# State-space steps and mLSTM steps of a hybrid token mixer in one loop

## The reference

```python
# SSD, per head: y = ((C B^T) * exp(segsum(a))) xc + C state * exp(a_cum)
#                state = state * exp(a_total) + B^T (decay * x)
# mLSTM, per head: m_t = max(b + m0, max(Dm)); W = exp(Dm - m_t)
#                num = (q k^T * W) v + (q C0) * exp(b + m0 - m_t); h = num / max(|den|, exp(-m_t))
#                C, n, m carried on to the next chunk
```

## Time and profile before

| | us |
|---|---|
| median of 3 runs | 4205.56 (4199.91 to 4212.05) |
| the profiled execution, own time | 4204.44 |
| its span | 4202.7 |
| PE / PEld / DVE / ACT busy | 3844.1 / 3257.1 / 2863.1 / 1994.6 |
| mean granted TensorE clock | 0.949 of full speed |

### The profile page before, as it was taken

The page is one execution under the profiler, slowest core; times in us unless marked ns, Lnnn a source line. Parts: engine busy times, 40 slices in busy tenths (PEclk is TensorE's granted clock), DMA queues, the critical chain, the costliest instruction groups (busy, mean ns, idle before and its releaser), DMA issues. The chain is left out here.

```text
span 4202.7 us, 61275 instructions
## 1 busy us (share of the span) xinstructions
PE 3844.1 (91%) x22686; PEld 3257.1 (78%) x22686; DVE 2863.1 (68%) x5816; ACT 1994.6 (47%) x4063; POOL 0.2 (0%) x4
## 2 busy tenths in 40 slices
PE   7999749989999999999999999989759899977998
PEld 4884547778887689999997788868449788867887
DVE  2535564348986868888768766654565499888666
ACT  2243213236666755555556544434224466665443
POOL 0000000000000000000000000000000000000000
PEclk9999869999999999999999999989769999999999
DMA  4221202225564455565554466523005355622665
GB/s 169 72 71 60 98 0 84 100 86 180 183 184 138 135 165 182 184 185 184 183 183 131 140 190 190 161 88 117 0 0 183 119 182 182 186 82 86 189 189 165
DMA packets 142200, 568.35 MB, mean 135 GB/s; under 512 B 15808, under 2 KB 17344, under 8 KB 130240
## 3 DMA queue, kind: packets, MB, share of 16 engines
q1 hardware_dynamic: 142016, 566.14, 42.7%
HBM read 565.03 MB, written 1.05 MB: 135 GB/s over the span
## 5 line engine op out<-in xcount | busy, mean ns | idle before, releaser
L1081 ACT ACTIVATE high<-ring 128x512 fp32r<-128x512 f32 x1632 | 1028.3, 632 | 1031.1 <-PE ps L515 510.1
L1538 DVE TENSOR_TENSOR low<-ring,high 128x512 fp32r<-128x512 f32 x1632 | 1075.8, 688 | 294.1 <-ACT high L1081 282.9
L515 PE MATMUL ps<-h_pair,high 128*128 128x512 f32 x3456 | 1236.1, 400 | 31.7 <-DVE low L1538 30.9
L515 PE MATMUL ps<-h_pair,low 128*128 128x256 f32 x3456 | 970.7, 281 | 0.0
L515 PEld LDWEIGHTS ps<-h_pair,high 128*128 128x128 f32 x3456 | 652.4, 189 | 188.0 <-issue 12.7
L911 PE MATMUL ps<-wt,high 128*128 128x512 f32 x2048 | 713.1, 392 | 5.7 <-DVE low L1538 5.7
L515 PEld LDWEIGHTS ps<-h_pair,low 128*128 128x128 f32 x3456 | 655.4, 190 | 0.0
L913 PE MATMUL ps<-wt,low 128*128 128x256 f32 x2048 | 574.7, 281 | 0.0
L515 PE MATMUL ps<-arena 128*128 128x128 f32 (+8 forms) x2432 | 444.3, 340 | 125.4 <-ACT arena L1081 75.6
L1081 ACT ACTIVATE arena<-ps 128x256 f32<-128x256 f32 (+3 forms) x654 | 271.1, 425 | 514.8 <-PE ps L515 486.1
L515 PEld LDWEIGHTS ps<-arena 128*128 128x128 f32 (+2 forms) x2432 | 326.3, 211 | 218.8 <-issue 115.7
(11 more groups left out here) (171 smaller groups left out, 4442.2 us busy)
## 6 DMA issues: line engine op xcount, KB each, us to landing
ring<-u_in SPq DMA_DIRECT2D x384, 512.0 KB, 3.6
ring<-v_in SPq DMA_DIRECT2D x384, 512.0 KB, 3.6
ring<-win_in SPq DMA_DIRECT2D x56, 1024.0 KB, 4.8
ring<-wmod_in SPq DMA_DIRECT2D x24, 1024.0 KB, 5.0
ring<-wq_in SPq DMA_DIRECT2D x48, 512.0 KB, 3.6
ring<-wmod_in SPq DMA_DIRECT2D x48, 512.0 KB, 3.6
ring<-wbr_in SPq DMA_DIRECT2D x16, 768.0 KB, 4.2
ring<-wout_in SPq DMA_DIRECT2D x8, 1024.0 KB, 4.8
```

What stands on the lines that cost most here:

```text
L515: return pe.matmul(o, l_, r, start=first, stop=last)
L1081: return act.activation(o, i_, f, **kw_)
L1538: return dve.tensor_tensor(o, a, b, op)
```

## The change

The SSD step and the mLSTM step of the same tile and direction stand in one loop body on every engine.

- Buffers: the SSD scratch gets a place of its own behind that of mLSTM; `dmat` has two halves, one per group, and is multiplied in place (`mmat` is gone); mLSTM adds up in `ml_acc`, which lies over `mlT`; the modulation rows go to `modrow_late`. `mergedT`, `br_high` and two of the three `w_high` buffers move.
- TensorE's order of a step: cb, row, ml_row, ml_qk, first half of modulation row A, ssd_dst, second half of A (and the turn of the row before), ssd_off, ml_int, ssd_y, first half of row B, ml_wT, second half of B, ml_num, ml_dst. `ssd_dst` is two products of 256 columns, each into 64 partitions of one half bank, in place of one of 512; so the state is read in two whole instructions in place of four half ones.
- ScalarE makes the SSD decays itself: relu(cm - row), four per group with a per-partition bias, then exp(-x). It takes the mLSTM exponentials in four pieces with the negative maximum as bias. It copies row A before the mLSTM exponentials, row B at the end of the step.
- VectorE multiplies `cb` by a 0/1 triangle as it reads it, has neither L1751 nor the subtraction on `rD`, and fewer instructions of 4 columns: the maxima carried from step to step are rearranged.
- The `ssd_dst` input `xd` is made first in the step.
- After the loop: both norms together, with one small instruction for all tiles where there were one per tile; the first gate slot is split at once, the second and third among the norms. The transposes of SSD come after the first gate slot's products, those of mLSTM after the second's. `br_high` of the attention follows the first slot's sigmoids, that of SSD the SSD transposes, that of mLSTM the second slot.

```diff
+        mergedT = view(scr_at, KB, T)
...
+        modrow_late = view(shapes_at + C_COS - C_KEPT, 2, 256)
...
+        ml_acc = view(s_mlT, NT, 512)
...
+        s_ssd = s + 4112
+        s = s_ssd
+        xc, xd, dmat, cb = view(s, 512), view(s + 512, 512), view(s + 1024, 2, 512), view(s + 2048, 256)
...
+        w_high = [rounded(f"w_high{r_}", w_, SLOT) for r_, w_ in enumerate((s_ssd, s_ssd + SLOT, merge_at))]
...
+                def rest_of_mod(n, hf):
                     if l == 0:
+                        w = slot(start["mod_rest", 0] - MOD_FIRST + n).rearrange("p (k m) -> p k m", k=KB)
+                        if hf == 0:
+                            row_bank[0] = claim("mod_row", 0, n)
+                        for k in range(4 * hf, 4 * hf + 4):
+                            i = mm(row_bank[0][0:2, 0:256], csil[:, k, :], w[:, k, :], k == 0, k == KB - 1)
+                        if hf:
+                            i.then_inc(*inc("mod_row", 0, n))
+                            if n > MOD_FIRST:
+                                mod_turn(0, n - 1, mod_bank[0], modrow_late)
...
+                            rest_of_mod(MOD_FIRST + 2 * (d * NT + n), 0)
+                        if kept_on:
+                            b = claim("ssd_dst", l, d, n)
+                            pe.wait_ge(*at("ssd_xd", l, d, n))
+                            pe.wait_ge(*at("B_t_read", l))
+                            for g in range(2):
+                                gp = slice(g * SN, g * SN + SN)
+                                i = mm(b[gp, 0:256], B_tm[:, t, gp], xd[:, g * 256:(g + 1) * 256])
+                            i.then_inc(*inc("ssd_dst", l, d, n))
+                        if shown:
+                            rest_of_mod(MOD_FIRST + 2 * (d * NT + n), 1)
...
+                            rest_of_mod(MOD_FIRST + 2 * (d * NT + n) + 1, 0)
                             b = claim("ml_wT", l, d, t)
                             pe.wait_ge(*at("ml_qk_read", l, d, t))
                             for h in range(MH):
                                 i = pe.transpose(b[:, h * P:(h + 1) * P], rW[:, h * P:(h + 1) * P], ident)
                             i.then_inc(*inc("ml_wT", l, d, t))
+                            rest_of_mod(MOD_FIRST + 2 * (d * NT + n) + 1, 1)
...
+                        if pr == 0 and q == 0:
+                            turn_out("ssd_T", "ssd_norm", acc)
+                        if pr == 0 and q == 1:
+                            turn_out("ml_T", "ml_norm", ml_acc)
...
+                            for g in range(2):
+                                b = bank("ssd_row", l, d, t, g)
+                                if shown_before:
+                                    act.wait_ge(*at("ssd_mm", l, *shown_before, g))
+                                for j in range(4):
+                                    h = d * 8 + g * 4 + j
+                                    i = fn(dmat[:, g, j * P:(j + 1) * P], b[:, j * P:(j + 1) * P], ACT.Relu,
+                                           scale=-1.0, bias=cm[:, t, h:h + 1])
+                                i.then_inc(*inc("ssd_row_read", l, d, t, g))
                             for g in range(2):
                                 act.wait_ge(*at("ssd_row_read", l, d, t, g))
+                                fn(dmat[:, g, :], dmat[:, g, :], ACT.Exp, scale=-1.0).then_inc(*inc("ssd_L", l, d, t, g))
+                            shown_before = d, t
+                            late_row(MOD_FIRST + 2 * (d * NT + n))
                             act.wait_ge(*at("ml_d", l, d, t))
+                            for h in range(MH):
+                                i = fn(rW[:, h * P:(h + 1) * P], rD[:, h * P:(h + 1) * P], ACT.Exp,
+                                       bias=sml[:, 0, 1, h:h + 1])
+                            i.then_inc(*inc("ml_w", l, d, t))
...
+                act.wait_ge(*at("ssd_y_read", l, 1, ORDER[1][-1]))
+                split_high(merge_item(l, 0))
...
+                        if pr == 0 and q == 1:
+                            branch_high(0, attT)
+                            branch(1, ssdT, "ssd_T", V_SSDN)
+                        if pr == 0 and q == 3:
+                            branch(2, mlT, "ml_T", V_MLN)
...
+                            if n or d:
+                                dve.wait_ge(*at("ssd_dst", l, *((d, n - 1) if n else (0, NT - 2))))
+                            tt(xd.rearrange("p (h e) -> p h e", h=SH), xs3, over(dw[:, t, dh], SD), ALU.mult
+                               ).then_inc(*inc("ssd_xd", l, d, n))
...
+                                tt(cb[:, g * P:(g + 1) * P], b[:, 0:P], tri[d], ALU.mult
+                                   ).then_inc(*inc("ssd_cb_read", l, d, t, g))
...
+                        if kept_on:
+                            i = dve.tensor_reduce(mloc, rows, AX.X, ALU.max)
+                        if shown:
+                            i = tt(rD3, rows, rep(nmask[1 - d], 4), ALU.add)
+                        i.then_inc(*inc("ml_row_read", l, d, t))
+                        dve.wait_ge(*at("ml_row_read", l, d, t))
+                        if shown:
+                            link(dve.tensor_reduce(rneg, rD3, AX.X, ALU.max, negate=True))
+                            link(dve.scalar_tensor_tensor(out=nm, in0=m_now, scalar=-1.0, in1=rneg, op0=ALU.mult,
+                                                          op1=ALU.min))
+                            tt(wi, m_now, nm, ALU.add)
+                            tt(en, nm, cm[:, t, fc], ALU.subtract).then_inc(*inc("ml_d", l, d, t))
+                            dve.wait_ge(*at("ml_d", l, d, t))
+                        if kept_on:
+                            link(tt(mmax, mloc, m_now, ALU.max))
+                            tt(ap_, m_now, mmax, ALU.subtract)
+                            tt(wk, rr[:, t, rc], mmax, ALU.subtract).then_inc(*inc("ml_g", l, d, n))
+                            dve.wait_ge(*at("ml_g", l, d, n))
+                            link(tt(m_now, mmax, cums[:, 2, t, fc], ALU.add))
...
+                                d3 = dmat[:, g, :].rearrange("p (a b) -> p a b", a=4)
+                                tt(d3, d3, rep(cb[:, g * P:(g + 1) * P], 4), ALU.mult
+                                   ).then_inc(*inc("ssd_m", l, d, t, g))
+                            dve.wait_ge(*at("ml_w", l, d, t))
+                            b = bank("ml_qk", l, d, t)
+                            tt(rW, b[:, :], rW, ALU.mult).then_inc(*inc("ml_qk_read", l, d, t))
...
+                split_low(merge_item(l, 0))
+                if l == 0:
+                    modulation(0, 1, ps[cnt.bank("mod", 0, 1)], MOD_FIRST, MOD_SLOTS)
+                scale_of(l, 32, scale2, V_N2)
...
+                split_low(merge_item(l, 1))
...
```

More of the change, by code:

```diff
@@ L210, in write_program @@
         dw = take(NT, 16)
-        etot = take(NT, 16)
+        etot = take(NT, 2, 4)
         negA = take(16)
@@ new lines, in _, with branch @@
+                fn(rinv[:, ts, 4:8], rinv[:, ts, 4:8], ACT.Sqrt).then_inc(*inc("ml_std", l))
+                split_high(merge_item(l, 2))
+                def branch(r, o, topic, col):
+                    act.wait_ge(*at(topic, l, outs(l)[-1]))
+                    for t in outs(l):
+                        b = bank(topic, l, t)
+                        for j in range(4):
+                            i = fn(o[:, j, t * P:(t + 1) * P], b[:, j * P:(j + 1) * P], ACT.Copy,
+                                   scale=vec[:, l, col + j:col + j + 1])
+                        i.then_inc(*inc(topic + "_read", l, t))
+                    act.wait_ge(*at(topic + "_read", l, outs(l)[-1]))
+                    branch_high(r, o)
@@ L1763, in _ @@
-                            first = d == 0
-                            if first:
+                        b = bank("ml_row", l, d, t)
+                        rows = b[:, :].rearrange("p (a b) -> p a b", a=4)
+                        if kept_on:
+                            i = dve.tensor_reduce(mloc, rows, AX.X, ALU.max)
+                        if shown:
+                            i = tt(rD3, rows, rep(nmask[1 - d], 4), ALU.add)
+                        i.then_inc(*inc("ml_row_read", l, d, t))
@@ L1803, in _ @@
-                if l == 0:
-                    modulation(0, 1, ps[cnt.bank("mod", 0, 1)], MOD_FIRST, MOD_SLOTS)
-                scale_of(l, 32, scale2, V_N2)
-                for t in outs(l):
-                    if t == outs(l)[0]:
-                        dve.wait_ge(*at("ssd_y_read", l, 1, ORDER[1][-1]))
-                        for n in range(2):
-                            dve.wait_ge(*at("z_read", l, n, 2))
-                    tt(acc[:, t, :], acc[:, t, :], z[:, t, :], ALU.mult).then_inc(*inc("ssd_yz", l, t))
-                    dve.wait_ge(*at("ssd_yz", l, t))
@@ L1929, in _ @@
-                    dve.wait_ge(*at("ml_std", l, t))
-                    link(dve.reciprocal(rinv[:, t, 0:4], rinv[:, t, 0:4]))
```

(14 more changed lines are left out.)

351 lines of the change are left out of this document (125 added, 226 removed).

## The result

The changed kernel takes 4014.53 us (median of 4 runs, 4009.59 to 4022.59) where the kernel before took 4203.24 beside it (4 runs, 4199.91 to 4212.05). The ratio of the times is 0.9547, with a 95% interval of 0.9525 to 0.9568: faster by 188.7 us. Timed a second time it took 4017.19 (5 runs, 4014.75 to 4032.24) against 4206.45, ratio 0.9549 [0.9536, 0.9562]. The forecast was 4034, its range with the first rival 4006 to 4092, and its own range 4012 to 4074.

What follows compares the result with a forecast made beforehand. TensorE was taken to set the time, with SSD and mLSTM filling each other's waits. Gains of 106.2 us (layer 0) and 64.9 (layer 1), sum 171.1 off 4204.4, gave 4034; own range 4012 to 4074, chance 0.80.

Steps and rivals of the forecast that it cites:

- the first rival: Merged steps have a longer period; each microsecond costs 8 + 4, four of them 48, giving 4082 us; chance 0.11.
- TensorE as the bound of layer 0: Merged step in layer 0: PE is the fuller engine, 18.7 us of work against VectorE's 16.0, period 19.9.
- The half microsecond of allowance per step: Layer 0 loop: 0.5 us per step for handovers left out of the order, taking 150.3 us to 154.3.
- The rival of a low clock: PE stays at 1.2 GHz, a layer 0 step takes 38.3 us; total 4193, no change to be told; chance 0.04.
- Layer 1: Merged loop of layer 1: 81 us at high clock, 100 at low, 93 taken; stage 101.5 for 166.4, gain 64.9.
- Behind the loops: After the loop: gate products 2.4 us later, then 4.4 us more in layer 0 and 2.5, 1.3 and 1.5 in layer 1.
- The short stall ahead of the SSD transposes: After the loop, PE's stall and SSD transposes: 2.3 us behind layer 0's first-slot products, 2.5 in layer 1.
- Relu: ScalarE's decays in shown steps: possible table loads of 1.28 us cost nothing in most steps, at worst 31 us.
- The DMA queue: Layer 0 loop: 16 MB of modulation weights have some 154 us, so SP's queue is no bound.
- The three handovers with little to spare: Merged step: weights for `rW`, ml_dst, and row A before the mLSTM exponentials each have under a microsecond to spare.
- the serial chain: Waits close into a chain, no engine overlaps another; a layer 0 step costs 42.7 us; total 4300, slower; chance 0.02.
- The fourth rival: The loops don't interleave and only the gaps behind them shrink (12 + 13 in layer 0, 8 + 6 in layer 1): 4165; chance 0.03.

Runs made afterwards that it cites:

- experiment 3: Changed kernel with ScalarE taking the mLSTM exponentials first and copying modulation row A after them: 4016.25 us, ratio 0.9552 to the kernel before.
- Experiment 7: Changed kernel with VectorE waiting for its own instruction before the next one inside the loop: 4032.31 us, ratio 0.9600 to the kernel before.
- experiment 4: Changed kernel with six of eight products of each late modulation row left out in layer 0: 4009.70 us, ratio 0.9545 to the kernel before.

## Why the prediction was right, and where its sizes were off

**TensorE as the bound of layer 0** held. A middle step has 19.01 us of PE in 19.43; the terms gave 18.7 and a period of 19.9. The order was read rightly too: a wait ahead of `ssd_y` for `rW` (0.42 us, 0.85 given), one of VectorE for `ml_dst` (3.79, some 3 given), none for the decays. The wait for the mLSTM weights is 1.0 instead of 0.35, which is row A's copy (experiment 3), and costs 2.5 us. VectorE's 16.0 us were 14.2 and 0.4 of links between them: a row of freely following instructions is shorter than its links of 0.03 us said. Experiment 7 gives back 7.7 us of busy time, 1.0 per step; the other 0.4 per step wasn't traced. With this the loop takes 147.0 for 154.3. The half microsecond of allowance per step wasn't needed.

**The clock** was 1.00 in the loop of layer 0, with an idle 0.42 us per step, through seven rotating banks. The rival of a low clock, which the Trainium skill's TensorE: Matmul & The Clock Gate, "A second HAM failure mode: psum-queue depth-cycling", would have made the forecast by my reading, did not come. That section speaks of a clock that goes back and forth, not of one that stays low, so the price of 4193 was harsher than what it says. The danger isn't free of ground: experiment 4 shows the loop at 0.88, with single steps between 0.75 and 1.00, once the wait is 1.93.

**Layer 1** is the term that was mis-sized: 93 us taken, 77.0 measured, below even the 81 at full clock (82 by its own terms, 9.5 + 2 x 18.1 + 2 x 11.5 + 11 + 2.4; nothing hangs on the slip). Two causes. First VectorE: with self-waits the loop takes 85.8 us (experiment 7), so 8.8 of the 16 are the overlap of its instructions. A step without output takes 5.03 us at the full clock where 6.4 were given, a shown one with n = 2 15.59 where 18.1 were. Second the clock: 0.84, where I took something between 0.65 and full. Weighing my own ends of 81 and 100 by 0.84 would have given 87. Windows of 7 us through the loop:

```profile
2876.00:2883.00 7.00, 6.22 (x52) 5.42 (x52) 5.89 (x14) 3.21 (x10) 0.00 (x0) 1.00 0.00 0
2883.00:2890.00 7.00, 5.39 (x45) 4.72 (x42) 6.66 (x18) 2.61 (x9) 0.00 (x0) 1.00 0.00 0
2890.00:2897.00 7.00, 6.42 (x53) 5.53 (x51) 6.64 (x19) 3.21 (x10) 0.00 (x0) 1.00 0.01 2
2897.00:2904.00 7.00, 4.99 (x23) 4.62 (x24) 5.12 (x11) 2.51 (x8) 0.00 (x0) 0.60 0.00 1
2904.00:2911.00 7.00, 4.84 (x21) 3.75 (x21) 5.36 (x17) 0.21 (x1) 0.00 (x0) 0.50 0.00 0
2911.00:2918.00 7.00, 5.78 (x32) 4.53 (x30) 5.03 (x16) 0.21 (x1) 0.00 (x0) 0.68 0.01 2
2918.00:2925.00 7.00, 6.18 (x50) 5.11 (x48) 5.83 (x18) 4.61 (x17) 0.00 (x0) 1.00 0.00 0
```

The shown steps with n = 2 run at 2.4 GHz. The last step of each direction (n = 3) begins at 2.4 GHz and ends at 1.2. The steps without output run at 2.4 GHz where they open the first direction and at 1.2, until the second one's end, where they open the second. The first fall comes as PE waits 1.91 us ahead of the `ssd_y` of the last step of the first direction, the second behind a wait of 1.73 us at the same place of the other direction:

```profile
2898.32 2.03 PE L521 MATMUL ps<-arena 128*128 128x64 f32 x9 [1.91 <-DVE arena L1575]
...
2937.89 2.25 PE L521 MATMUL ps<-arena 128*128 128x64 f32 x16 [1.73 <-DVE arena L1575]
```

The two levels were expected, but not that the fullest steps would hold the higher one.

**Behind the loops** the terms held: 2.4 and 2.3 us to the gate products (2.4 given), then 4.1 more than before until the first branch product in layer 0 (4.4 given) and 4.8 in layer 1 (5.3). The short stall ahead of the SSD transposes is absent: PE takes all transposes of layer 0 in 3.8 us with no idle time, those of layer 1 in 2.1 where 3.8 were given, and the fourth slot there is late by 1.9 where 1.5 was given.

**Relu** needs no table load; the two that remain in the stage are those of the norms, outside the loop. **The DMA queue** is no bound: 0.33 of its share in the loop.

**The rivals.** The three handovers with little to spare didn't add up to a longer period; the serial chain and the low clock stayed away. The fourth rival, that the scans don't interleave, would not have cost what I gave it: with the scans apart the kernel takes 4115, not 4165, since the rest of the change, priced there at the gaps of 39 us alone, is worth 92. So the sum of 171.1 had the right terms and two of them too small, layer 1 by 16.5 us of stage gain and layer 0 by 6.5. The 194.1 us of the stages are even 1.6 more than the low ends of both layers together gave (115.6 + 76.9); so the profiled execution (4009.6) lies outside the forecast's own range of 4012 to 4074, and the median inside it by 2.5 us.

**Against the median.** The stages gave 194.1 us and the medians 188.7 and 189.3. The profiled execution of the changed kernel was the fastest of nine. In the one other that has a profile the stretches outside the change were 23.0 us longer; for the remaining seven that is likely and not shown.

## What to carry to other kernels

Put two independent chains into one loop when the engines of one idle while those of the other work. Filled gaps paid twice here, as idle time and as clock (17 of 57 us in layer 0, 21 of 44 in layer 1). Size such a loop by two figures: the work of the fullest engine (19.0 of 19.4 us) and the handovers between the engines (15.9 us when PE had 13.6 of work). A next cut in work pays only down to the second, and it can cost clock: in experiment 4, 42.6 us of TensorE's products went and 16.2 came out. Move work off the engine that carries the chain even if the other engine is no faster at it, and leave out every wait of VectorE for itself that its data don't need.

## What the hardware showed beside that

- One program has two rates in the expert stretch, in windows with PE busy all of the time at a granted clock of 1.00: 579 products in 100 us or 567, and 189 GB/s or 187. It changes from execution to execution and from layer to layer: of eleven profiles of the changed kernel and its variants, five have 2318 to 2319 us between the layers, one 2321.6, and five 2325 to 2328. The one profile of before has 2315.6. What chooses the rate is open, and so is whether the kernel before meets the slower one as often; if it didn't, part of the 5 us between stages and medians would be this.
- In the small input products of layer 0 (32 columns each) the granted clock of a window in which PE never idles is 0.73 in one execution and 0.59 in the other, 129 and 116 products in 25 us. That makes up most of the 3.5 us at the start.
